# The last norm of a hybrid decoder step: scale per token at the eviction, and the second MLP's input written row by row

## The chip, the cores and the metric

The kernel runs on one core of a Trainium2 chip. TensorE (PE) multiplies, VectorE (DVE), ScalarE (ACT) and GpSimd (POOL) work on elements, SyncE (SP) issues most of the DMAs. The metric is the time of one execution on the device in microseconds; lower is better.

## The reference

One inference step of a decoder with two layers, 512 prompt tokens and 8 sample tokens, model width 1024, MLP width 4096. Layer 0 mixes with a gated linear recurrence, layer 1 with sparse attention. What the change touches is the MLP of layer 1 and the final norm:

```python
def rmsnorm(x, g):
    xf = x.astype(jnp.float32)
    y = xf * lax.rsqrt(jnp.mean(xf * xf, axis=-1, keepdims=True) + RMS_EPS)
    return (y * g.astype(jnp.float32)).astype(x.dtype)

def sq_relu_mlp(h, w_up, w_down):
    return jnp.square(jax.nn.relu(h @ w_up)) @ w_down

# per layer:
x = x + o                                             # o: the mixer's output
x = x + sq_relu_mlp(rmsnorm(x, norm_mlp[l]), w_mlp_up[l], w_mlp_down[l])
# at the end:
return rmsnorm(x, norm_final), ...
```

## The kernel before, in words

The stream x lies transposed in SBUF: 128 partitions, KD = 8 rows, N = 520 columns. Row k holds features 128k to 128k+127, a column is a token (512 of the prompt, 8 samples). A sum over the features of a token is thus a sum over rows and partitions.

A dense product (dense, L869; chunk_products, L858) goes by chunks of 128 output features. TensorE takes slabs of 2 MB of weights from stream, which SP loads two ahead, and adds up over the input rows in PSUM, in two halves of 260 columns; even chunks use banks 0 and 1, odd ones banks 2 and 3 (pair, L116). A matmul of float32 is two records in the trace. chunk_ready counts finished chunks, chunk_taken those that VectorE has taken out. The second MLP's up product has 32 chunks of 8 rows, the down product 8 chunks of 32 rows; both run in loops on TensorE and VectorE.

A norm goes as follows. residual (L1962) adds a chunk to its row of x on VectorE. Behind each row ScalarE writes its square into scratch (norm_act, L1447); GpSimd adds the squares of the first seven rows into the first (squares_added, L685); TensorE multiplies that row and the last one with a matrix of ones (norm_sum, L843), so that each partition holds the sum of every token in banks 6 and 7. ScalarE takes the root of mean plus eps (L1462), VectorE its reciprocal over 128 by 520 elements (norm_dve, L1825): rstd. At an MLP the product runs on rows that carry the gain alone (gained, L1442), and rstd is applied when the product is evicted (squared_relu, L1973). The rows with the gain are written by ScalarE either behind each square ("early", the first MLP) or all eight behind the last square ("late", the second MLP, into h, which the output projection nsa_out still reads until its last chunk).

At the end VectorE writes h = x * gain * rstd (L2314). TensorE turns h by 128 by 128 transposes, 4 to a PSUM bank, into token-major tiles (L1422; u counts 8 tiles: four blocks of 128 tokens, first for features 0 to 511, then for 512 to 1023; banks 0 to 3 in turn), the samples by 8 more (L1425). VectorE evicts even tiles (L2319), ScalarE odd ones (L1796). SP issues the first half of the output when four tiles are out, the second when eight are, then the samples (L613 to L621).

Each engine runs its own list in order and waits on semaphores; the order is written out by hand.

## Time and profile before

| what | value |
|---|---|
| median of 3 runs | 2174.71 us (2173.55 to 2177.26) |
| the profiled execution's own time | 2175.39 us |
| its span, first to last instruction | 2173.6 us |
| mean granted clock of TensorE | 0.967 |
| PE busy | 2030.5 us (93%) |
| DVE, ACT, POOL busy | 611.9, 404.6, 362.3 us (28%, 19%, 17%) |
| chain that ended last: TensorE's share | 85% |

The span is what the trace covers; the time of a run holds a little around it. The chain is followed back from the last instruction, at each step to what released it. A granted clock of 1.00 is 2.4 GHz, of 0.50 is 1.2 GHz. A page's line gives source line, engine, operation, tiles written and read.

### The profile page before, as it was taken

To read this page: it belongs to the slowest core of one execution; us is meant where nothing else is said; L and a number is where in the kernel's file an instruction comes from. 1 tells how busy PE (TensorE), PEld (TensorE's weight loads), DVE (VectorE), ACT (ScalarE), POOL (GpSimd) and SP (SyncE) were. 2 spreads that over 40 slices of the span, in tenths; PEclk is the share of its full clock that TensorE was granted. 3 is DMA by queue.
4 is the path that set the end of the run, shared out by engine and by line. 5 is a ranking of instruction groups with operands and counts; after the bars stand their busy time and mean duration, and the time that the engine had idled before them with its cause. 6 is when DMAs were issued, how large, how long until landed. Compare 5 with 4: busy or idle time off the path is not lost.

```text
span 2173.6 us, 28193 instructions
## 1 busy us (share of the span) xinstructions
PE 2030.5 (93%) x11084; PEld 1694.9 (78%) x11084; DVE 611.9 (28%) x1085; ACT 404.6 (19%) x839; POOL 362.3 (17%) x575
## 2 busy tenths in 40 slices
PE   7999998899999999999779999799849999999997
PEld 6888887788888888888656668687428788888886
DVE  3555456212211000011237753334401222110002
ACT  3343444210000000100225533233300100000000
POOL 2323234100000000000036654341011000000000
PEclk9999999899999999999859999899979999999999
DMA  5322232012222223215350009887991122212221
GB/s 137 87 62 63 68 100 70 22 66 77 77 77 77 77 77 77 77 43 193 73 143 2 2 1 221 183 184 202 293 323 70 39 77 77 69 47 77 77 77 39
DMA packets 213834, 206.83 MB, mean 95 GB/s; under 512 B 13906, under 2 KB 167107, under 8 KB 213603
## 3 DMA queue, kind: packets, MB, share of 16 engines
q1 hardware_dynamic: 195970, 186.84, 30.9%
q10 hardware_dynamic: 16416, 14.95, 2.1%
q0 software_dynamic: 1344, 3.67, 0.5%
q8 instruction: 64, 1.05, 0.2%
q14 instruction: 40, 0.32, 0.1%
HBM read 194.33 MB, written 18.42 MB: 98 GB/s over the span
## 4 chain that ended last, share of the span: by engine, by line
PE 85%; DVE 3%; SPq 3%; DMA 3%; ACTq 2%; issue 2%; ACT 2%; POOL 1%; DVEq 0%; POOLq 0%
PE ps L865 52%; PE ps L904 11%; PE ps L1083 4%; PE ps L1076 2%; PE ps L944 2%; DMA stream<-in_cache_nsa_kv 2%; PE ps L919 1%; PE ps L1137 1%; PE ps L1159 1%; ACTq L1715 1%; PE ps L1177 1%; PE ps L1285 1%; ACTq L347 1%; PE ps L970 1%; SPq L562 1%
## 5 line engine op out<-in xcount | busy, mean ns | idle before, releaser
L865 PE MATMUL ps<-h,stream 128*128 128x260 f32 x2688 | 593.4, 384 | 5.8 <-ACT h L1444 4.1
L865 PEld LDWEIGHTS ps<-h,stream 128*128 128x128 f32 x2688 | 512.8, 191 | 85.9 <-issue 4.7
L865 PE MATMUL ps<-big,stream 128*128 128x260 f32 (+1 forms) x2464 | 544.6, 384 | 4.7 <-DVE big L1981 3.9
L865 PEld LDWEIGHTS ps<-big,stream 128*128 128x128 f32 (+1 forms) x2464 | 468.0, 190 | 81.0 <-issue 5.1
L904 PE MATMUL ps<-h,stream 128*128 128x260 f32 x1024 | 237.0, 386 | 5.1 <-DVE h L1836 5.1
L904 PEld LDWEIGHTS ps<-h,stream 128*128 128x128 f32 x1024 | 191.7, 192 | 37.2 <-issue 10.0
L1453 ACT ACTIVATE scratch<-x 128x520 f32<-128x520 f32 x32 | 20.4, 637 | 1039.0 <-DVE x L1969 1039.0
L692 POOL TENSOR_TENSOR scratch<-scratch 128x520 f32<-128x520 f32 x24 | 30.9, 1285 | 995.8 <-ACT scratch L1453 995.8
L1969 DVE TENSOR_TENSOR x<-x,ps 128x520 f32 x32 | 22.3, 696 | 538.5 <-PE ps L865 522.8
L1978 DVE SCALAR_TENSOR_TENSOR scratch<-ps,rstd 128x520 f32<-128x520 f32 x64 | 44.8, 700 | 344.8 <-PE ps L865 344.8
L1083 PE MATMUL ps<-big 128*128 128x256 f32 x384 | 99.7, 383 | 0.0
L722 POOL COPY scratch<-stream 128x512 f32<-128x512 f32 (+1 forms) x72 | 43.2, 616 | 257.2 <-DMA stream<-big 157.4
L2151 DVE COPY big<-ps 128x512 f32<-128x512 f32 x80 | 55.3, 691 | 101.1 <-PE ps L1076 77.3
L1635 ACT ACTIVATE big<-ps,scratch 128x128 f32<-128x128 f32 (+3 forms) x128 | 66.3, 526 | 84.8 <-DVE scratch L2072 84.8
L746 POOL TENSOR_SCALAR big<-big,scratch 128x128 f32<-128x128 f32 (+3 forms) x128 | 77.2, 613 | 26.1 <-DVE scratch L2078 26.1
L1883 DVE COPY_PREDICATED scratch<-scratch,ps 128x512 f32<-128x512 int32 x64 | 47.0, 735 | 122.0 <-PE ps L944 100.6
L1685 ACT ACTIVATE big<-ps 128x512 f32<-128x512 f32 x81 | 48.4, 597 | 129.8 <-PE ps L1076 93.5
L1083 PEld LDWEIGHTS ps<-big 128*128 128x128 f32 x384 | 66.0, 192 | 5.4 <-DVE big L2151 0.3
L944 PEld LDWEIGHTS ps<-scratch 128*128 128x128 f32 x448 | 59.8, 199 | 9.8 <-POOL scratch L676 5.2
L944 PE MATMUL ps<-scratch 128*128 128x128 f32 x448 | 62.7, 285 | 3.7 <-POOL scratch L676 3.7
L675 POOL TENSOR_TENSOR scratch<-scratch,stream 128x256 f32<-128x256 f32 x56 | 46.0, 822 | 115.3 <-ACT stream L1521 101.2
L1076 PE MATMUL ps<-ident,scratch 128*128 128x128 f32 (+1 forms) x288 | 45.8, 288 | 16.8 <-POOL scratch L722 16.7
(311 smaller groups left out, 2000.4 us busy)
## 6 DMA issues: line engine op xcount, KB each, us to landing
stream<-in_w_mlp_up SPq DMA_DIRECT2D x16, 2048.0 KB, 7.6
stream<-in_w_mlp_down SPq DMA_DIRECT2D x16, 2048.0 KB, 9.0
stream<-in_cache_nsa_kv SPq DMA_DIRECT2D x128, 256.0 KB, 6.1
stream<-in_w_hgrn_in SPq DMA_DIRECT2D x32, 512.0 KB, 7.0
stream<-in_cache_nsa_kv SPq DMA_DIRECT2D x114, 128.0 KB
stream<-in_cache_nsa_kv ACTq DMA_DIRECT2D x114, 128.0 KB
stream<-in_cache_win_kv SPq DMA_DIRECT2D x16, 512.0 KB
out<-in_cache_win_kv SPq DMA_DIRECT2D x8, 1022.0 KB
```

The lines of the kernel that those rows point to most:

```text
L675: nc.gpsimd.tensor_tensor(lv[:, :, 0, :], kv[:, :, 0, :], ev[:, :, 0, :], ALU.mult)
L746: nc.gpsimd.tensor_scalar(probs, probs, wts[u % 4][:, br:br + 1], gtok[:, t, gate:gate + 1], ALU.mult, ALU.mult).then_inc(pa["probs"], 1)
L865: m = nc.tensor.matmul(pair(c)[0:n1, a, :], w[:, k, P * c_local:P * c_local + n1], rhs[:, k, NH * a:NH * a + NH], start=(k == 0), stop=(k ...
L904: m = nc.tensor.matmul(pair(c)[:, a, :], w[:, k, :], h[:, k, NH * a:NH * a + NH], start=(k == 0), stop=(k == KD - 1))
L944: m = nc.tensor.matmul(ps[:, 5 - l % 2, P * c:P * c + P], Lv[l % 2][:, P * c:P * c + P], Lv[l % 2][:, P * c:P * c + P], start=True, stop=True)
L1076: m = nc.tensor.transpose(ps[:, bank, P * g:P * g + n], src[0:n, g, :], ident[0:n, 0:n])
L1083: m = nc.tensor.matmul(ps[:, bank, 0:G * n // 2], W1[kv][:, kk, :, :].rearrange("p a n -> p (a n)"), columns(par), start=(rp == 0 and par ...
L1635: m = nc.scalar.activation(Pb[u % 4][:, br, 0:w], ps[:, 2 * a + br, 0:w], ACT.Exp, bias=nmax[a][:, br:br + 1], accum_out=sums[u % 4][:, br ...
L1685: nc.scalar.activation(out, ps[:, TB[s % 3], :], ACT.Copy).then_inc(sm["ev0"], 1)
L1883: nc.vector.copy_predicated(AT.rearrange("p (c t) -> p c t", c=TT), masks[:, mask:mask + 1, :].to_broadcast([P, TT, P]).bitcast(I32), ps[: ...
L1978: nc.vector.scalar_tensor_tensor(out=halves(Mz[p]), in0=pair(c), scalar=0.0, in1=halves(rstd[:]), op0=ALU.max, op1=ALU.mult).then_inc(relu ...
L2151: nc.vector.tensor_copy(out, ps[:, TB[s % 3], :]).then_inc(sm["ev1"], 1)
```

## The change

For the second MLP, the rows with the gain are written behind each square, into a buffer of their own in scratch (mlp_in), which the up product reads in place of h. The squares no longer lie in eight rows of scratch but in one row that gathers the sum, a ring of two, and one for the last row; ScalarE therefore waits, from the fourth row on, until GpSimd has added the row before last (square_taken).

For the final norm, the rows with the gain alone are written into h behind each square. TensorE sums the squares with the row of squares as the stationary operand and one column of ones, so that the sum of a token stands on the partition of that token (4 columns for the prompt's blocks, one for the samples): first for the row that GpSimd has added up, then for the last. VectorE copies the first into SBUF and adds the second, ScalarE takes the root, VectorE the reciprocal, of 128 by 4 and 8 by 1 elements. The transposes wait for the rows of h alone; tiles 0 to 3 go to banks 4 to 7, tiles 4 to 7 to banks 2, 3, 0, 1. The scale of a token is applied when its tile is evicted, and the samples' eviction is split between VectorE and ScalarE.

```diff
--- before.py
+++ after.py
@@ -256,6 +256,11 @@
         out_count = {"mix0": KD, "mlp0": 2 * KD, "kv": 3 * KD, "attn": 4 * KD, "mlp1": 5 * KD, "final": 6 * KD}
         squares = scratch[:, 0:KD * N].rearrange("p (k t) -> p k t", k=KD)
         squares_in = big[:, 12:12 + KD, :]
+        mlp_in = scratch[:, 0:KD * N].rearrange("p (k t) -> p k t", k=KD)
+        sq_total, sq_last = scratch[:, KD * N:KD * N + N], scratch[:, at_end - 5 * T + 2 * N:at_end - 5 * T + 3 * N]
+        sq_ring = [scratch[:, KD * N + N * n:KD * N + N * n + N] for n in range(1, 3)]
+        square_rows = [sq_total] + [sq_ring[k % 2] for k in range(1, KD - 1)] + [sq_last]
+        token_rstd = small[:, 0:TT + 1]
 
         per_head = {
             "in_min": 1, "in_sp": 1, "lf": 1, "f": 1, "th": 1, "g": 1, "scan": 1, "k": 1, "dend": 1, "d": 7, "take": 8,
@@ -300,7 +305,13 @@
         block = ctx.enter_context(nc.Block())
 
         hready = sem("hready")
-        ydone, ysdone = [sem("ydone0"), sem("ydone1")], sem("ysdone")
+        ydone, ysdone = [sem("ydone0"), sem("ydone1")], [sem("ysdone0"), sem("ysdone1")]
+        square_taken, token_scale = sem("square_taken"), sem("token_scale")
+        token_part, token_added = sem("token_part"), sem("token_added")
+
+        def y_bank(u):
+            return 4 + u if u < TT else (2 + u - TT) % 4
+
         yturned = sem("yturned")
         yrows = big[:, 0:8, :].rearrange("p k t -> p (k t)")[:, 0:TT * D].rearrange("p (a n) -> p a n", a=TT)
         ysrows = big[0:B, 8:10, :].rearrange("p k t -> p (k t)")[:, 0:D]
@@ -617,7 +628,8 @@
                     sp.wait_ge(ydone[p], TT // 2 * (half + 1))
                 sp.dma_start(y_prompt[0].rearrange("(a p) n -> p a n", p=P)[:, :, D // 2 * half:D // 2 * half + D // 2],
                              yrows[:, :, D // 2 * half:D // 2 * half + D // 2]).then_inc(stored, 16)
-            sp.wait_ge(ysdone, 1)
+            for p in range(2):
+                sp.wait_ge(ysdone[p], 1)
             sp.dma_start(y_sample.rearrange("b a n -> (b a) n"), ysrows).then_inc(stored, 16)
             for p in range(2):
                 sp.wait_ge(s0_out[p], 16 * heads // 2)
@@ -817,7 +829,14 @@
                     page, = page_numbers(mybir.EngineType.Pool, first_page(i, j) + 3, 1)
                     nc.gpsimd.dma_start(kv_tile(i)[:, j, 3, :], page_rows(i, j, page)).then_inc(pool_in[kv_slot(i)], 16)
 
-            squares_added("mlp1")
+            n = turn_of["mlp1"]
+            pool.wait_ge(norm["sq"], n * KD + 1)
+            for k in range(1, KD - 1):
+                pool.wait_ge(norm["sq"], n * KD + k + 1)
+                m = nc.gpsimd.tensor_tensor(sq_total, sq_total, square_rows[k], ALU.add)
+                m.then_inc(square_taken, 1)
+                pool.wait_ge(square_taken, k)
+            pool.sem_inc(norm["added"], 1)
             squares_added("final")
 
 
@@ -1404,23 +1423,46 @@
             pe.wait_ge(hready, 8)
             pe.wait_ge(pa["out"], UNITS)
             dense("nsa_out", 2, h, KD, 512)
-            norm_sum("mlp1", squares)
+            n = turn_of["mlp1"]
+            pe.wait_ge(norm["added"], n)
+            for a in range(2):
+                nc.tensor.matmul(ps[:, 6 + a, 0:NH], ones[:], sq_total[:, NH * a:NH * a + NH], start=True, stop=False)
+            pe.wait_ge(norm["sq"], n * KD + KD)
+            for a in range(2):
+                m = nc.tensor.matmul(ps[:, 6 + a, 0:NH], ones[:], sq_last[:, NH * a:NH * a + NH], start=False, stop=True)
+            m.then_inc(norm["sum"], 1)
             pe.wait_ge(norm["out"], out_count["mlp1"])
-            dense("up1", 8, h, KD, 512, turns=4)
+            dense("up1", 8, mlp_in, KD, 512, turns=4)
             for p in range(2):
                 pe.wait_ge(chunk_taken[p], taken(p, chunk_base["down1"]))
             dense("down1", 8, big, KF, P, turns=4)
-            norm_sum("final", squares)
-
+            def token_sums(k):
+                for a in range(TT + 1):
+                    n1 = min(P, N - P * a)
+                    m = nc.tensor.matmul(ps[0:n1, k % 2, a:a + 1], squares[:, k, P * a:P * a + n1], ones[:, 0:1],
+                                         start=True, stop=True)
+                return m
+
+            n = turn_of["final"]
+            pe.wait_ge(norm["added"], n)
+            pe.wait_ge(chunk_taken[0], taken(0, chunk_base["down1"] + KD))
+            token_sums(0).then_inc(token_part, 1)
+            pe.wait_ge(norm["sq"], n * KD + KD)
+            token_sums(KD - 1).then_inc(norm["sum"], 1)
+
+            pe.wait_ge(norm["out"], out_count["final"] - 1)
             for u in range(2 * TT):
                 a, cg = u % TT, u // TT
-                if a == 0:
-                    pe.wait_ge(norm["out"], out_count["final"] - KD // 2 * (1 - cg))
-                if u >= 4:
-                    pe.wait_ge(ydone[u % 2], (u - 4) // 2 + 1)
+                if u == TT:
+                    pe.wait_ge(norm["out"], out_count["final"])
+                    pe.wait_ge(chunk_taken[1], taken(1, chunk_base["down1"] + KD))
+                    pe.wait_ge(token_added, 1)
                 for c in range(4):
-                    m = nc.tensor.transpose(ps[:, u % 4, P * c:P * c + P], h[:, 4 * cg + c, P * a:P * a + P], ident[:])
+                    m = nc.tensor.transpose(ps[:, y_bank(u), P * c:P * c + P], h[:, 4 * cg + c, P * a:P * a + P], ident[:])
                 m.then_inc(yturned, 1)
+            for p in range(2):
+                pe.wait_ge(ydone[p], 1)
             for c in range(KD):
                 m = nc.tensor.transpose(ps[0:B, 4 + c // 4, P * (c % 4):P * (c % 4) + P], h[:, c, T:N], ident[:])
             m.then_inc(yturned, 1)
@@ -1789,12 +1831,33 @@
                     for c in range(3):
                         load_page(i, j, c)
 
-            norm_act("mlp1", squares, added("nsa_out"), late=[(GAIN_MLP + KD, h)])
-            norm_act("final", squares, added("down1"))
+            n, wait_row = turn_of["mlp1"], added("nsa_out")
+            for k in range(KD):
+                wait_row(k)
+                if 3 <= k < KD - 1:
+                    act.wait_ge(square_taken, k - 2)
+                nc.scalar.activation(square_rows[k], x[:, k, :], ACT.Square).then_inc(norm["sq"], 1)
+                gained(GAIN_MLP + KD, mlp_in, k)
+            act.wait_ge(norm["sum"], n + 1)
+            nc.scalar.activation(halves(rstd[:]), ps[:, 6:8, 0:NH], ACT.Sqrt, bias=eps[:], scale=1.0 / D)\
+                .then_inc(norm["sqrt"], 1)
+
+            n, wait_row = turn_of["final"], added("down1")
+            for k in range(KD):
+                wait_row(k)
+                nc.scalar.activation(squares[:, k, :], x[:, k, :], ACT.Square).then_inc(norm["sq"], 1)
+                gained(GAIN_FINAL, h, k)
+            act.wait_ge(token_added, 1)
+            nc.scalar.activation(token_rstd[0:B, TT:TT + 1], token_rstd[0:B, TT:TT + 1], ACT.Sqrt, bias=eps[0:B], scale=1.0 / D)
+            nc.scalar.activation(token_rstd[:, 0:TT], token_rstd[:, 0:TT], ACT.Sqrt, bias=eps[:], scale=1.0 / D)\
+                .then_inc(norm["sqrt"], 1)
+            act.wait_ge(token_scale, 1)
             for u in range(1, 2 * TT, 2):
                 act.wait_ge(yturned, u + 1)
-                nc.scalar.activation(yrows[:, u % TT, 512 * (u // TT):512 * (u // TT) + 512], ps[:, u % 4, :], ACT.Copy)\
-                    .then_inc(ydone[1], 1)
+                nc.scalar.activation(yrows[:, u % TT, 512 * (u // TT):512 * (u // TT) + 512], ps[:, y_bank(u), :], ACT.Copy,
+                                     scale=token_rstd[:, u % TT:u % TT + 1]).then_inc(ydone[1], 1)
+            act.wait_ge(yturned, 2 * TT + 1)
+            nc.scalar.activation(ysrows[:, D // 2:D], ps[0:B, 5, :], ACT.Copy, scale=token_rstd[0:B, TT:TT + 1]).then_inc(ysdone[1], 1)
 
 
         @block.vector
@@ -2309,17 +2372,23 @@
             norm_dve("mlp1")
             squared_relu("up1")
             residual("down1")
-            norm_dve("final")
-            for k in range(KD):
-                nc.vector.scalar_tensor_tensor(out=h[:, k, :], in0=x[:, k, :],
-                                               scalar=vec[:, GAIN_FINAL + k:GAIN_FINAL + k + 1], in1=rstd[:],
-                                               op0=ALU.mult, op1=ALU.mult).then_inc(norm["out"], 1)
+            dve.wait_ge(token_part, 1)
+            nc.vector.tensor_copy(token_rstd[0:B, TT:TT + 1], ps[0:B, 0, TT:TT + 1])
+            ch.link(nc.vector.tensor_copy(token_rstd[:, 0:TT], ps[:, 0, 0:TT]))
+            dve.wait_ge(norm["sum"], turn_of["final"] + 1)
+            nc.vector.tensor_tensor(token_rstd[0:B, TT:TT + 1], token_rstd[0:B, TT:TT + 1], ps[0:B, 1, TT:TT + 1], ALU.add)
+            nc.vector.tensor_tensor(token_rstd[:, 0:TT], token_rstd[:, 0:TT], ps[:, 1, 0:TT], ALU.add).then_inc(token_added, 1)
+            dve.wait_ge(norm["sqrt"], turn_of["final"] + 1)
+            nc.vector.reciprocal(token_rstd[0:B, TT:TT + 1], token_rstd[0:B, TT:TT + 1])
+            ch.link(nc.vector.reciprocal(token_rstd[:, 0:TT], token_rstd[:, 0:TT]))
+            dve.sem_inc(token_scale, 1)
             for u in range(0, 2 * TT, 2):
                 dve.wait_ge(yturned, u + 1)
-                nc.vector.tensor_copy(yrows[:, u % TT, 512 * (u // TT):512 * (u // TT) + 512], ps[:, u % 4, :])\
-                    .then_inc(ydone[0], 1)
+                nc.vector.tensor_scalar(yrows[:, u % TT, 512 * (u // TT):512 * (u // TT) + 512], ps[:, y_bank(u), :],
+                                        token_rstd[:, u % TT:u % TT + 1], None, ALU.mult).then_inc(ydone[0], 1)
             dve.wait_ge(yturned, 2 * TT + 1)
-            nc.vector.tensor_copy(ysrows.rearrange("p (c n) -> p c n", c=2), ps[0:B, 4:6, :]).then_inc(ysdone, 1)
+            nc.vector.tensor_scalar(ysrows[:, 0:D // 2], ps[0:B, 4, :], token_rstd[0:B, TT:TT + 1], None, ALU.mult)\
+                .then_inc(ysdone[0], 1)
 
 
 # ---- launch: one core; inputs and outputs as the reference has them ----
```

ScalarE's list from the last chunks of nsa_out to the first square of the down product, before (scratch takes the squares):

```order
L1453 ACTIVATE scratch<-x 128x520 [waits chunk_taken1]
L1453 ACTIVATE scratch<-x 128x520 [waits chunk_taken0]
L1444 ACTIVATE h<-x,vec 128x520 x8
L1462 ACT_TABLE_LOAD
L1462 ACTIVATE rstd<-ps,eps 128x520 [waits norm_sum]
L1453 ACTIVATE scratch<-x 128x520 [waits chunk_taken1]
```

And after, where scratch takes the squares and, with vec as second operand, the rows with the gain:

```order
L1839 ACTIVATE scratch<-x 128x520 [waits square_taken,chunk_taken0]
L1486 ACTIVATE scratch<-x,vec 128x520
L1839 ACTIVATE scratch<-x 128x520 [waits square_taken,chunk_taken1]
L1486 ACTIVATE scratch<-x,vec 128x520
L1839 ACTIVATE scratch<-x 128x520 [waits chunk_taken0]
L1486 ACTIVATE scratch<-x,vec 128x520
L1842 ACT_TABLE_LOAD
L1842 ACTIVATE rstd<-ps,eps 128x520 [waits norm_sum]
L1848 ACTIVATE scratch<-x 128x520 [waits chunk_taken1]
L1486 ACTIVATE h<-x,vec 128x520
```

The eight scaled rows that stood together behind the last square now stand one behind each square, and the squares from the fourth to the seventh wait for square_taken too.

VectorE's list from the end of the last product's loop to the end of the kernel, before:

```order
L1964 COMPARE_AND_BRANCH
L1827 RECIPROCAL rstd<-rstd 128x520 [waits norm_sqrt,chunk_taken1,chunk_taken0]
L2314 SCALAR_TENSOR_TENSOR h<-x,vec,rstd 128x520 [waits dve_chain]
L2314 SCALAR_TENSOR_TENSOR h<-x,vec,rstd 128x520 x7
L2319 COPY big<-ps 128x512 [waits yturned] x4
L2322 COPY big<-ps 8x1024 [waits yturned]
```

And after (stream is the buffer that holds the small per-token numbers):

```order
L2027 COMPARE_AND_BRANCH
L2376 COPY stream<-ps 8x1 [waits token_part,chunk_taken1,chunk_taken0]
L2377 COPY stream<-ps 128x4
L2379 TENSOR_TENSOR stream<-stream,ps 8x1 [waits norm_sum,dve_chain]
L2380 TENSOR_TENSOR stream<-stream,ps 128x4
L2382 RECIPROCAL stream<-stream 8x1 [waits norm_sqrt]
L2383 RECIPROCAL stream<-stream 128x4
L2387 TENSOR_SCALAR big<-ps,stream 128x512 [waits dve_chain,yturned]
L2387 TENSOR_SCALAR big<-ps,stream 128x512 [waits yturned] x3
L2390 TENSOR_SCALAR big<-ps,stream 8x512 [waits yturned]
```

The reciprocal over 520 columns and the eight scaled rows are gone; six instructions on one or four columns stand in their place, and the evictions read a scale.

TensorE's list from the end of the last product, before:

```order
L854 MATMUL ps<-scratch,ones 128x260 [waits norm_added]
L854 MATMUL ps<-scratch,ones 128x260
L854 MATMUL ps<-scratch,ones 128x260 [waits norm_sq]
L854 MATMUL ps<-scratch,ones 128x260
L1422 MATMUL ps<-ident,h 128x128 [waits norm_out]
L1422 MATMUL ps<-ident,h 128x128 x15
L1422 MATMUL ps<-ident,h 128x128 [waits ydone0,norm_out]
L1422 MATMUL ps<-ident,h 128x128 x3
L1422 MATMUL ps<-ident,h 128x128 [waits ydone1]
```

And after:

```order
L1443 MATMUL ps<-ones,scratch 128x1 [waits chunk_taken0,norm_added]
L1443 MATMUL ps<-ones,scratch 128x1 x3
L1443 MATMUL ps<-ones,scratch 8x1
L1443 MATMUL ps<-ones,scratch 128x1 [waits norm_sq]
L1443 MATMUL ps<-ones,scratch 128x1 x3
L1443 MATMUL ps<-ones,scratch 8x1
L1462 MATMUL ps<-ident,h 128x128 [waits norm_out]
L1462 MATMUL ps<-ident,h 128x128 x15
L1462 MATMUL ps<-ident,h 128x128 [waits token_added,chunk_taken1,norm_out]
L1462 MATMUL ps<-ident,h 128x128 x15
L1467 MATMUL ps<-ident,h 8x128 [waits ydone1,ydone0]
L1467 MATMUL ps<-ident,h 8x128 x7
```

The sums are ten matmuls of one column, in place of four of 260; of the transposes, none waits for an eviction except those of the samples.

## Rows read from the trace of the kernel before

**Rows 1.** The chain of waits, 1690 us to the end: start us, us, what.

```profile
1690.92 0.64 ACT scratch L1453
1691.56 4.96 ACT h L1444 x8
...
1696.84 226.39 PE ps L865 x1024
...
1925.14 226.39 PE ps L865 x1024
...
2152.41 0.65 ACT scratch L1453
...
2153.09 1.16 PE ps L854 x4
...
2154.28 0.70 ACT rstd L1462
...
2155.46 3.41 DVE rstd L1827
...
2158.90 2.79 DVE h L2314 x4
...
2161.73 5.31 PE ps L1422 x32
```

**Rows 2.** Timeline, first MLP and second: start us, us, instruction [idle before <-releaser].

```profile
460.41 0.64 ACT L1453 ACTIVATE scratch<-x 128x520 f32<-128x520 f32 x1 [5.76 <-DVE x L1969]
460.95 0.71 ACT L1444 ACTIVATE h<-x,vec 128x520 f32<-128x520 f32 x1
461.10 1.15 PE L854 MATMUL ps<-scratch,ones 128*128 128x260 f32 x4 [0.70 <-ACT scratch L1453]
462.08 8.30 PE L865 MATMUL ps<-h,stream 128*128 128x260 f32 x37
469.31 0.70 DVE L1978 SCALAR_TENSOR_TENSOR scratch<-ps,rstd 128x520 f32<-128x520 f32 x1 [2.11 <-PE ps L865]
...
1705.84 0.70 DVE L1978 SCALAR_TENSOR_TENSOR scratch<-ps,rstd 128x520 f32<-128x520 f32 x1 [3.79 <-PE ps L865]
```

**Rows 3.** Stretches: us, then each engine's busy us; PEclk, DMA share, GB/s.

```profile
462.00:464.00 2.00, 2.00 (x11) 1.77 (x10) 0.20 (x1) 1.66 (x2) 0.00 (x0) 1.00 1.05 401
...
1696.80:1698.00 1.20, 1.16 (x3) 0.97 (x4) 0.00 (x0) 1.19 (x2) 0.00 (x0) 0.61 0.00 0
...
1925.20:1927.00 1.80, 1.80 (x6) 1.45 (x7) 0.00 (x0) 0.00 (x0) 0.00 (x0) 0.65 1.13 333
...
2161.70:2163.70 2.00, 1.97 (x9) 1.98 (x10) 2.00 (x4) 0.00 (x0) 0.00 (x0) 0.50 0.00 0
2164.70:2166.70 2.00, 2.00 (x19) 1.80 (x18) 1.60 (x4) 1.09 (x2) 0.00 (x0) 1.00 0.00 0
2166.60:2172.40 5.80, 1.31 (x13) 0.87 (x10) 1.90 (x2) 0.80 (x2) 0.00 (x0) 0.92 1.00 367
```

**Rows 4.** Timeline of SyncE, the issues of the output's two halves.

```profile
2165.82 2.31 SPq L618 DMA_DIRECT2D out<-big  x2
```

**Rows 5.** Groups by line and shape: xcount | busy us, mean ns | idle before.

```profile
L1010 PE MATMUL ps<-big,stream 128*128 128x1 f32 x128 | 15.1, 248 | 0.0
...
L944 PE MATMUL ps<-scratch 128*128 128x128 f32 x448 | 62.7, 285 | 3.7 <-POOL scratch L676 3.7
...
L985 PE MATMUL ps<-ident,scratch 128*128 128x128 f32 x32 | 4.8, 272 | 0.0
...
L1433 ACT ACTIVATE lnb<-lnb 128x8 f32<-128x8 f32 x1 | 0.2, 209 | 9.4 <-DVEq L1810 9.4
...
L1843 DVE TENSOR_SCALAR big<-ps 128x520 f32<-128x520 f32 x8 | 5.5, 694 | 4.8 <-PE ps L904 4.8
...
L2078 DVE RECIPROCAL scratch<-scratch 128x2 f32<-128x2 f32 x64 | 10.6, 165 | 23.4 <-POOL scratch L741 21.3
...
L692 POOL TENSOR_TENSOR scratch<-scratch 128x520 f32<-128x520 f32 x24 | 30.9, 1285 | 995.8 <-ACT scratch L1453 995.8
```

## The prediction

> **What bounds the kernel now.** I read the chain of waits from its end backwards, then the timeline of the two places that the change touches, then the granted clock there, and last the durations of single instructions.
>
> The chain [rows 1] shows TensorE as the bound nearly everywhere: the second MLP's two products take 226.39 us each without a break (1024 records each, so 0.221 us a record, and with 32 chunks 7.07 us a chunk). Two stretches on it have no product running, and the change is about these.
>
> The first lies before the second MLP. The last residual row is squared at 1690.92; then ScalarE writes all eight rows of the MLP's input (4.96 us), and only at 1696.84 does TensorE start [rows 1]. The first MLP of the kernel, at 460 us, has the other order: there each row of input is written right behind its square, so that behind the last square one row is left. Square at 460.41, product at 462.08 [rows 2]. That is the very form the change brings to the second MLP, so the trace of before shows its price.
>
> The second is the end. Behind the last square at 2152.41 come: sums by TensorE (1.16), square root (0.70), reciprocal over 520 columns (3.41), eight rows scaled, of which the first four must be there (2.79), 32 transposes (5.31), with their evictions [rows 1]. The first half of the output is issued at 2165.82 [rows 4]. From 2166.6 to 2172.4 the DMA share is 1.00 at 367 GB/s [rows 3]: 2.1 MB of output at that rate are 5.8 us, that is, the tail is full of transfer from the moment that the first half is issued, and the span ends 2173.6 - 2165.8 = 7.8 us after that issue. So what the end is worth is read from one instant: when the first half is issued.
>
> **The change, part by part.** Times are those of the profiled execution, span 2173.6, its own time 2175.39; that is 0.7 over the median of the runs (2174.71).
>
> *Inputs of the second MLP.* Seven of eight scaled rows leave the stretch behind the last square; they stand behind the seven earlier squares, where ScalarE has 7.07 us a chunk and needs 0.64 + 0.71 [rows 1, 2]. The new buffer lets these rows be written while the products of the output projection still read h. The added wait of ScalarE on GpSimd's additions costs nothing: rows come 7.07 us apart, an addition takes 1.29 [rows 5], and three rows may be open; behind the waiting square stands only that chunk's scaled row. The price is read off the first MLP: from last square to first eviction of the up product 469.31 - 460.41 = 8.90 us; in the second 1705.84 - 1690.92 = 14.92 us [rows 1, 2]. Difference 6.02. It has two parts. The start: 1.67 against 5.92, that is 4.25. And the clock: in the first MLP TensorE pauses 0.70 us before the sums and stays at 1.00 (2.4 GHz); in the second it has been idle since its sums (they end 1.84 us behind the square by the first MLP's rows, so at 1692.8) and is granted 0.61 in the first 1.2 us of the product [rows 2, 3], and the first chunk takes 1.8 us longer. I take all 6.0. Bounds: 4.25 if the clock falls here as well, 6.0 if not. The reciprocal is late next: sums, table, root and 3.41 us of reciprocal begin as early as in the first MLP, where the first eviction waited for the product, not for it.
>
> *The last norm.* The scaled rows (plain gains now, without the norm) move behind each square, where a chunk of the down product is 226.39 / 8 = 28.3 us long: nothing on the path. The seven earlier rows are summed while the last product still runs. What is left behind the last square's end, 2153.05:
> - token sums of the last row: 5 matmuls of one column, 10 records at 15.1 / 128 = 0.118 us [rows 5], with the start 1.3 us: 2154.4;
> - two small additions, two small square roots, two small reciprocals: four on VectorE at 0.165, two on ScalarE at 0.21 [rows 5], with three handovers of some 0.05: 1.2 us: 2155.6. Before, VectorE issued its reciprocal 0.48 us after the root's end at 2154.98 [rows 1]; I leave 0.4 for such a late issue: 2156.0;
> - meanwhile TensorE goes on from the sums into the transposes, which need only the plain rows, into banks that are free. At full clock 19 records fall in 2.0 us [rows 3], 0.105 each: 16 of them, and the drain, end at 2156.4, so that the third and fourth tile are there before their evictions are due;
> - evictions with the scale per token: VectorE 0.70 (a scaled copy from PSUM, [rows 5]), for ScalarE I take the 0.71 of a row scaled from SBUF [rows 2]. Two each: 2157.4, first half issued at 2157.5.
>
> That is 2165.8 - 2157.5 = 8.3 us earlier. The second half follows 1.5 us later, within the 2.9 us of transfer of the first, and the samples' rows (8 transposes and two evictions of eight partitions) come 2 to 3 us behind the first issue, still under the transfer: the tail keeps its 7.8 us. The removed reciprocal over 520 columns and the eight scaled rows on VectorE lay wholly on the path, the transposes too; they now lie beside the chain or are gone.
>
> The bounds of this part: 9 us if VectorE issues without the 0.4 and a hand-over is shorter; 5.5 us if sums and transposes all run at half clock (sums 2.6, transposes 0.22 each [rows 3], first issue at 2160.3).
>
> Of the clock in this stretch the rows speak both ways. After the pause of 0.7 us before the sums of the first MLP the product went on at 1.00 [rows 2, 3]; after the pause of 1.9 us between the two products of the second MLP (1696.84 + 226.39 = 1923.23 to 1925.14) they ran at 0.65 in the mean of 1.8 us [rows 1, 3]. After the change there are a pause of 0.7 and one-column matmuls on both sides of it. I take the full clock, and keep the fall as a rival. The transposes themselves ran at 0.50 after the long pause and were granted 1.00 while nothing but transposes was issued [rows 3]. The Trainium skill says otherwise ("TensorE: Matmul & The Clock Gate", Part 4: PE-mode transpose): the full clock does not engage for transposes. The row of 2164.7 to 2166.7 does not agree. By the page's rule the first issue would come at 2158.8, and the sum would be 1.3 us less.
>
> **Sum.** 6.0 + 8.3 = 14.3: 2175.4 - 14.3 = 2161.1 in the profiled execution's terms, 2160.4 against the median of the runs. I forecast 2161.0, between these.
>
> **Rivals.**
> - *The clock falls in the last stretch,* or VectorE's first instructions behind its loop come late. For it: the fall after 1.9 us, and the late issue of 0.48. Against it: 1.00 after the pause of 0.7. Price 1.3 (transposes alone at half clock: 16 at 0.22 from 2154.4, with drain and eviction, issue at 2158.8) to 2.8 (sums too): 2162.3 to 2163.8.
> - *The clock falls at the second MLP all the same:* 1.8 of the 6.0 is lost, 2162.8. The first MLP is the same sequence and shows 1.00 [rows 3].
> - *The up product becomes slower, and with it the kernel.* TensorE now streams its input from scratch, where VectorE writes the rectified rows at the same time, and not from h. It decides from 14.3 / 1024 = 14 ns a record; from 18 ns the kernel is slower by over 0.2%. For it: matmuls from scratch in the first layer took 285 ns in the mean where those with the identity took 272 [rows 5], 13 ns, with other engines writing there; that alone would give 2174.4, twice that 2187.7. Against it: the product from h, beside which VectorE writes scratch and big, and the one from big, beside which it writes x, take the same 226.39 to the digit [rows 1].
> - *No change that can be told:* only if 10 of the 14 us fail to come; the scratch rival at its half is the one way that I see.
>
> **How the numbers follow.** Forecast 0.58, the clock or a late issue in the last stretch 0.33, the clock at the second MLP 0.05, the slower product 0.04, of which half ends on the slow side. The forecast's own range, with 1.5 us of spread for a median of few runs (those of before lie between 2173.55 and 2177.26), is 2159 to 2163; with the first rivals 2158.3 to 2164.6, which leaves out under 2 in 10. Faster by over 0.2% (4.3 us, about what a measurement of this kernel can tell from no change) 0.96, within 0.2% 0.02, slower 0.02.
>
> **What would show it.** Second MLP: one scaled row on the chain behind the last square, its product within 2 us of that square, granted 1.00, and 226.4 us long; a longer product means the scratch rival. End: the first output issue 8 us closer to the last square than the 13.4 of before; the chain there going square, sums, small steps, evictions, DMA; transposes beginning at the end of the sums. A clock of 0.5 between the sums and the last transpose means the first rival. The forecast is wrong if the DMA tail takes longer than 7.8 us behind its first issue, or if the stretch up to 1690 us moves, where no instruction has changed.

## The result, and the profile after

The changed kernel took 2156.64 us (median of 4 runs, 2155.37 to 2161.49), the kernel before on the same chip 2174.19 (4 runs, 2173.55 to 2177.26): ratio 0.992, 95% interval 0.9906 to 0.9934. It is faster, by 17.6 us where 13.7 were forecast against the median shown (2174.71 to 2161.0); 2156.64 lies 2.4 below the forecast's own range (2159 to 2163) and 1.7 below the wider one (from 2158.3).

The profiled execution of the changed kernel took 2157.23, span 2155.6, mean granted clock 0.968, PE busy 2027.9 us (94%). Its chain of waits, in the stretches that [rows 1] show of before (start us, us, what):

```profile
1687.80 0.65 ACT scratch L1839
...
1688.48 1.14 PE ps L1432 x4
1689.63 224.46 PE ps L884 x1024
...
1916.00 224.70 PE ps L884 x1024
...
2140.85 0.71 DVE x L2032
2141.56 0.14 issue
2141.69 2.26 PE ps L1443 x20
2143.95 5.31 PE ps L1462 x32
```

Three things are to be seen against [rows 1]. From the last square to the up product it is now 1.83 us (5.92 before), and that product takes 224.46 (226.39). The down product takes 224.70 (226.39), though nothing of it was changed. And at the end the scaled rows, the long reciprocal and the matrix of ones are gone; token sums and transposes alone are left. But the last square itself comes at 1687.80 and not at 1690.92, behind instructions that are the same in both kernels.

The clock in these stretches (us, then each engine's busy us; PEclk, DMA share, GB/s), beside [rows 3]:

```profile
1689.60:1691.60 2.00, 2.00 (x11) 1.74 (x10) 0.41 (x1) 1.45 (x2) 0.00 (x0) 1.00 0.00 0
1916.00:1918.00 2.00, 2.00 (x9) 1.77 (x10) 0.00 (x0) 0.00 (x0) 0.00 (x0) 1.00 1.15 322
2141.60:2144.00 2.40, 2.31 (x21) 2.25 (x22) 0.22 (x2) 1.23 (x2) 0.00 (x0) 1.00 0.00 0
2144.40:2148.00 3.60, 3.60 (x20) 3.60 (x19) 1.83 (x5) 1.76 (x4) 0.00 (x0) 0.53 0.02 5
2148.60:2154.40 5.80, 1.53 (x15) 1.08 (x12) 1.54 (x3) 1.88 (x3) 0.00 (x0) 1.00 1.00 367
```

Both products of the second MLP begin at 1.00. Behind the token sums the transposes run at 0.53: the clock fell there, so 32 of them take 5.31 us as before. The last row is the output's transfer, full at 367 GB/s as before.

The timeline of SyncE answers to [rows 4], and that of ScalarE shows what the first half of the output waited for (start us, us, instruction [idle before <-releaser]):

```profile
2147.80 2.63 SPq L629 DMA_DIRECT2D out<-big  x2
```

```profile
2141.58 0.64 ACT L1848 ACTIVATE scratch<-x 128x520 f32<-128x520 f32 x1 [26.82 <-DVE x L2032]
...
2144.50 0.28 ACT L1852 ACTIVATE stream<-stream,eps 128x4 f32<-128x4 f32 x1
2145.40 0.69 ACT L1857 ACTIVATE big<-ps,stream 128x512 f32<-128x512 f32 x1 [0.61 <-PE ps L1462]
2147.05 0.69 ACT L1857 ACTIVATE big<-ps,stream 128x512 f32<-128x512 f32 x1 [0.96 <-PE ps L1462]
```

From the end of the last square (2142.22) to the first issue are 5.58 us; they were 12.77 (2153.05 to 2165.82). The second of ScalarE's two evictions waited 0.96 us for a transpose at half clock: that is the wait which now ends last. Behind the issue the span ends 7.80 us later (2155.6 - 2147.8), as before.

So the 18.0 us between the two spans come apart like this:

| stretch | before | after | gain | in the forecast |
|---|---|---|---|---|
| up to the last square before the second MLP | 1690.92 | 1687.80 | 3.1 | 0 |
| that square to the start of the down product | 234.22 | 228.20 | 6.0 | 6.0 |
| down product | 226.39 | 224.70 | 1.7 | 0 |
| its end to the first output issue | 14.29 | 7.10 | 7.2 | 8.3 |
| first issue to the end | 7.8 | 7.8 | 0 | 0 |

What has to be explained is two gains that no changed instruction made (4.8 together), and 1.1 us missing at the end.

### The profile page after: what moved, and what is told of

It is laid out like the page before. It is cut to its first block, busy times and chain, and to the rows that moved or that the text cites. A ratio compares the mean times of both kernels' runs of the same rounds, so it can differ in the third digit from the quotient of the medians.

```text
span 2155.6 us, 28235 instructions
## 1 busy us (share of the span) xinstructions
PE 2027.9 (94%) x11096; PEld 1692.9 (79%) x11096; DVE 603.6 (28%) x1082; ACT 410.3 (19%) x849; POOL 362.4 (17%) x575
## 4 chain that ended last, share of the span: by engine, by line
PE 85%; SPq 3%; DVE 3%; DMA 3%; ACTq 2%; issue 2%; ACT 1%; POOL 1%; DVEq 0%; POOLq 0%
PE ps L884 52%; PE ps L923 11%; PE ps L1102 4%; PE ps L1095 2%; PE ps L963 2%; DMA stream<-in_cache_nsa_kv 2%; ACTq L1757 1%; PE ps L938 1%; PE ps L1156 1%; PE ps L1178 1%; PE ps L1196 1%; PE ps L1304 1%; ACTq L358 1%; SPq L573 1%; PE ps L989 1%
## 5 line engine op out<-in xcount | busy, mean ns | idle before, releaser
L884 PE MATMUL ps<-h,stream 128*128 128x260 f32 x1664 | 367.0, 384 | 1.7 <-DVE h L2368 1.7
L884 PEld LDWEIGHTS ps<-h,stream 128*128 128x128 f32 x1664 | 317.1, 191 | 51.1 <-DVE h L2368 1.9
L923 PE MATMUL ps<-h,stream 128*128 128x260 f32 x1024 | 237.0, 386 | 5.1 <-DVE h L1899 5.1
L884 PE MATMUL ps<-scratch,stream 128*128 128x260 f32 x1024 | 224.6, 382 | 0.0
L923 PEld LDWEIGHTS ps<-h,stream 128*128 128x128 f32 x1024 | 191.7, 192 | 37.3 <-issue 10.0
L884 PEld LDWEIGHTS ps<-scratch,stream 128*128 128x128 f32 x1024 | 194.5, 190 | 30.0 <-issue 0.2
L704 POOL TENSOR_TENSOR scratch<-scratch 128x520 f32<-128x520 f32 x18 | 23.2, 1287 | 915.6 <-ACT scratch L1495 490.5
L1495 ACT ACTIVATE scratch<-x 128x520 f32<-128x520 f32 x16 | 10.2, 637 | 482.9 <-DVE x L2032 482.9
L1848 ACT ACTIVATE scratch<-x 128x520 f32<-128x520 f32 x8 | 5.1, 636 | 441.7 <-DVE x L2032 441.7
```

The source lines that it names most:

```text
L884: m = nc.tensor.matmul(pair(c)[0:n1, a, :], w[:, k, P * c_local:P * c_local + n1], rhs[:, k, NH * a:NH * a + NH], start=(k == 0), stop=(k ...
L923: m = nc.tensor.matmul(pair(c)[:, a, :], w[:, k, :], h[:, k, NH * a:NH * a + NH], start=(k == 0), stop=(k == KD - 1))
```

## Experiments

**Each half alone (E1, E2), and the changed kernel again.** E1 has the new second MLP and the old last norm, E2 the reverse (lines against the changed kernel, cut):

```diff
# E1: last norm as before
-            token_sums(0).then_inc(token_part, 1)
...
-            token_sums(KD - 1).then_inc(norm["sum"], 1)
+            norm_sum("final", squares)
# E2: second MLP as before
-            dense("up1", 8, mlp_in, KD, 512, turns=4)
+            dense("up1", 8, h, KD, 512, turns=4)
...
+            norm_act("mlp1", squares, added("nsa_out"), late=[(GAIN_MLP + KD, h)])
```

> Only the second MLP's part of the change: its inputs written behind each square; the last norm as before. Theory A (the time is the sum of the two edits, and what else the two traces differ by is chance of single executions): 6.0 us faster than before (4.3 from the earlier start of the up product, 1.8 from a clock that stays at 1.00 there), so 2168.2. Theory B (the change as a whole also quickens the stretch ahead of 1690 us or the down product, by 3 to 5 us, in every execution): 9 to 11 us faster if this part brings it, 6.0 if not. In its trace: up product 224.5 us, starting within 2 us of the last square; the last square of the output projection at 1690.9 by B's denial, at 1687.8 by B.

> Only the last norm's part: sums per token, scale at the eviction; the second MLP's inputs all behind the last square, as before. Theory A: 7.2 us faster than before (14.0 us from the last square to the end of the span against 21.2), so 2167.0, up to 8.5 where the clock does not fall in the transposes. Theory B: 10 to 12 us faster if this part brings the rest, 7.2 if neither alone does and only both together do. Up product 226.4 us as before, with the fall of the clock at its start.

> The changed kernel once more, with a new profile. Theory A (chance): the last square of the output projection lies anywhere between 1687 and 1692 us, as in the other runs whose instructions up to there are the same; the pause of 1.9 us between up and down product is followed by a low clock in some executions (down product 226.4) and not in others (224.7); the time against before 13.5 to 17.5 us faster. Theory B: 1687.8 and 224.7 again, 17.5 us faster.

On one chip, beside the kernel before at 2173.77 (16 runs, 2169.89 to 2177.93): E1 2166.62 (9 runs; ratio 0.9963, 0.9951 to 0.9974), E2 2166.54 (6 runs; 0.9968, 0.9957 to 0.998), the changed kernel 2159.1 (5 runs, 2156.44 to 2161.3; 0.9935, 0.9922 to 0.9947). The halves gain 7.15 and 7.23, 14.4 together; the whole gains 14.7. They add up as far as intervals of two to three us either way can tell. E1 alone does not decide between the theories: its last square came at 1686.38, the sign of theory B, and its interval, 5.7 to 10.7 us, holds A's 6.0 and reaches into B's 9 to 11. The changed kernel's second trace decides it for A, with a late square and a long down product:

```profile
1689.82 0.65 ACT scratch L1839
...
1691.65 224.46 PE ps L884 x1024
...
1918.02 226.39 PE ps L884 x1024
```

E1's chain, second MLP and the start of the old last norm:

```profile
1688.21 224.46 PE ps L877 x1024
...
1914.58 224.70 PE ps L877 x1024
...
2142.81 0.40 issue
2143.21 3.42 DVE rstd L1856
```

The up product from scratch takes 224.46 here too: the rival of a slower product has fallen. E2's end of chain:

```profile
2151.82 0.71 DVE x L2008
2152.53 0.14 issue
2152.66 2.26 PE ps L1429 x20
2154.92 5.22 PE ps L1448 x32
```

It is the same as in the changed kernel, with its first issue at 2159.19, 7.37 behind the last residual add (6.95 in the first trace of the changed kernel, 7.34 in the second, 14.14 before).

**Token sums before the last eviction (E3).** The 20 records of token sums stand in one piece, behind a wait for the residual add. Ten of them, of the first seven rows, were to run before it. They waited because the last chunk of the down product lies in banks 0 and 1 and the sums were written there. E3 puts them into banks 2 and 3, which are free a chunk earlier, and the late tiles into 0 to 3 in the other order:

```diff
-            return 4 + u if u < TT else (2 + u - TT) % 4
+            return 4 + u if u < TT else u - TT
...
-                    m = nc.tensor.matmul(ps[0:n1, k % 2, a:a + 1], squares[:, k, P * a:P * a + n1], ones[:, 0:1],
+                    m = nc.tensor.matmul(ps[0:n1, 2 + k % 2, a:a + 1], squares[:, k, P * a:P * a + n1], ones[:, 0:1],
```

> The changed kernel with one thing moved: the first token sums go to bank 2 and the last to bank 3, in place of banks 0 and 1, which the last chunk of the down product holds until VectorE has added it; tiles 4 to 7 go to banks 0 to 3. If the wait for that bank is what put both token sums on the path, TensorE starts the first ones right behind the product and the two are no longer one piece of 2.26 us: 0.8 to 1.1 us faster than the changed kernel, where the clock is the same in both. If the sums were hidden anyway, or the fall of the clock sets the transposes whatever the sums do, the same within 0.3 us.

2159.18 (6 runs; 0.9936, 0.9923 to 0.995): the same as the changed kernel beside it. TensorE's timeline:

```profile
2142.43 1.07 PE L1443 MATMUL ps<-ones,scratch 128*128 128x1 f32 x10
2144.18 1.18 PE L1443 MATMUL ps<-ones,scratch 128*128 128x1 f32 x10 [0.67 <-ACT scratch L1848]
2145.29 5.31 PE L1462 MATMUL ps<-ident,h 128*128 128x128 f32 x32
```

The first ten now stand right behind the product, as meant, but the transposes still take 5.31 us, and from residual add to first issue it is 6.89 (6.95). From the end of the product to the first issue it is 7.04 (7.10 to 7.49 in the changed kernel). The six runs spread too widely to tell a gain of 0.8; by the trace the bank was the reason of that wait, but not what the end was waiting for: that was the clock, as the next experiment shows.

**The clock held up by matmuls that nobody reads (E4, E4b).** E4 is E3 with two full matmuls behind the early sums; their result goes to bank 6, which nobody reads. E4b has two more ahead of the sums:

```diff
+            def keep_busy(count, row):
+                for n in range(count):
+                    nc.tensor.matmul(ps[:, 6, 0:NH], ones[:], row, start=True, stop=True)
...
             token_sums(0).then_inc(token_part, 1)
+            keep_busy(2, big[:, 20, 0:NH])
```

> The early sums of the run before, and two matmuls of 260 columns that no one reads between the first and the last token sums (0.9 us of TensorE, in a pause of 0.7: the last sums come some 0.25 us later). Theory C: the low clock in the transposes comes from the pause and the one-column matmuls ahead of them, and hides what the early sums gain. Then with the pause filled the clock holds 1.00 at least in a part of the executions, the transposes take 3.6 us in place of 5.2, the first output issue comes 6 us behind the last addition in place of 6.9, and the kernel is 0.5 to 1 us faster than the changed one. Theory D: the clock has no part in it, the evictions set the end: the same or 0.25 us slower.

> As the run before with two more such matmuls right behind the last product, ahead of the first token sums: TensorE is then busy with wide matmuls in 1.8 of the 3 to 4 us ahead of the transposes, and the last sums come 1.1 us later. Theory C: granted clock 1.00 from the product to the last transpose, transposes 3.5 us, first issue some 6.6 us behind the last addition. Theory D: transposes at 0.50 for part of the way as in the four traces with the new norm, first issue at 8.

E4's chain:

```profile
2144.29 0.91 PE ps L1448 x10
2145.20 1.07 PE ps L913 x4
2146.28 0.91 PE ps L1448 x10
2147.19 3.64 PE ps L1468 x32
```

Its first output issue, by SyncE's timeline:

```profile
2149.88 2.12 SPq L629 DMA_DIRECT2D out<-big  x2
```

The clock in the two stretches, sums and transposes:

```profile
2144.30:2147.20 2.90, 2.90 (x24) 2.70 (x25) 0.91 (x3) 1.25 (x2) 0.00 (x0) 1.00 0.01 3
2147.20:2150.80 3.60, 3.60 (x34) 3.56 (x35) 2.80 (x8) 2.55 (x5) 0.00 (x0) 1.00 0.02 5
```

All 32 transposes run at 1.00 in 3.64 us, and from the end of the product to the first issue it is 5.59 (2149.88 - 2144.29) where the changed kernel needs 7.10 to 7.49. So 1.5 to 1.9 us of the end were the clock and the bank together, and 1.45 of it came with the two filling matmuls (7.04 in E3): theory C. They fill the pause and stand among the one-column matmuls at once, so which of the two brings the fall is not separated. The Trainium skill says that the full clock does not engage for transposes ("TensorE: Matmul & The Clock Gate", Part 4: PE-mode transpose); the second row does not agree, since nothing but transposes was issued in it.

The time shows little of this: E4 2157.28 (5 runs; 0.9922, 0.991 to 0.9935), E4b 2158.19 (one run). The two further matmuls of E4b buy nothing: transposes 3.65, from the product's end to the first issue 6.47. E4's profiled execution took 2159.29, 2 us more than that of the changed kernel, because its last square before the second MLP came at 1691.37. What varies there hides what is gained here.

**The pause between the products (E5), and the kernel before again.** In [rows 3] the clock fell behind the 1.9 us pause between up and down product. E5 fills it, in both layers alike, with three matmuls that nobody reads (the second layer's is shown):

```diff
             dense("up1", 8, mlp_in, KD, 512, turns=4)
+            keep_busy(3, big[:, 0, 0:NH])
```

> The changed kernel with three matmuls of 260 columns that no one reads (1.3 us) in the pause of 1.9 us between up and down product of both MLPs. Theory E: whether the clock falls behind that pause is chance of the execution, 1.7 us each time (seen in 4 of 6 traces at each of the two places). Filled, the down products take 224.7 us in every execution, the clock never falls there, and the kernel is 2.3 us faster in the mean than the changed kernel (2 places x 1.7 x 4 of 6). If the fall has another cause than the pause, the same.

> The kernel before once more, for a second trace. Theory A (the stretch up to the last square of the output projection differs by chance): anywhere between 1686 and 1692 us. Theory B (the new second MLP quickens it): 1690.9 or later again, as in the two traces with the old second MLP, against 1686.4 to 1689.8 in the four with the new one.

E5: 2157.14 (6 runs, 2154.65 to 2163.41; 0.9934, 0.9919 to 0.9948). In its trace the clock falls behind neither up product, and the down product takes 224.70. The 2.3 us of theory E do not show in the times: the changed kernel was not run beside it, and its ratio to before was 0.9935 both in its second and in its third measurement. Nor are the runs closer together: the slowest two (2162.36 and 2163.41) had a mean granted clock of 0.966 and 0.964 over the whole execution, the fastest three 0.971. Either the fill does not hold in every execution or the clock, and the time with it, varies elsewhere as well; with one trace that is open. Without a fill the fall is a matter of the single execution. Over ten traces without it, the pause in the second layer was followed by a low clock and a down product of 226.38 or 226.39 us in six (both of before, E2, the changed kernel's second, E3, E4b), and by 1.00 and 224.69 or 224.70 in four (the changed kernel's first and third, E1, E4). In the first layer, where not one instruction was touched and the pause is 2.0 us, it fell in eight of the ten (not in E1 and E3).

The kernel before, taken again, has its last square at 1689.33, which theory B excluded, and a time of 2174.24.

**All three together (E6), beside the changed kernel a third time.** E6 has E3's banks, E4's two matmuls, E5's three (the first line below stands behind up0 and behind up1):

```diff
+            keep_busy(3, big[:, 0, 0:NH])
...
             token_sums(0).then_inc(token_part, 1)
+            keep_busy(2, big[:, 20, 0:NH])
```

> The three pieces of E3, E4 and E5 together: token sums into banks 2 and 3, two filling matmuls behind the sums of the first seven rows, three filling matmuls in the pause between up and down product of both layers. Theory A (the granted clock is what is left to gain behind the change): TensorE at 1.00 from the first MLP to the last transpose; the down product 224.5 to 224.7 in every execution (226.4 where the clock falls), 32 transposes 3.64 and not 5.3, from the end of the down product to the first output issue 5.5 and not 6.9 to 7.3. Against the changed kernel on the same chip 1.3 from the end and 1 to 2 from the product boundary of the second layer, 0 to 2 from that of the first: 2.3 to 4 us less, median some 2155.5 if the changed kernel has 2158.5. Theory B (the pieces overlap, or each filling matmul costs what it gives back): within 1 us of the changed kernel.

> The changed kernel unchanged, a third time, beside E6 on the same chip. If the unchanged stretch in front of the second MLP differs by chance from execution to execution: last square of the output projection anywhere between 1685 and 1691.5, the median between 2156 and 2160. If the change itself moved that stretch forward by 3 us: square below 1689.

E6 2155.72 (6 runs, 2154.09 to 2159.54; 0.9917, 0.9904 to 0.993), the changed kernel 2161.09 (6 runs, 2156.38 to 2162.44; 0.9935, 0.9922 to 0.9949), the kernel before 2174.96 (11 runs). Between the means of six runs each, 2156.36 and 2160.52, lie 4.2 us; the runs' own spread (standard deviations 2.0 and 2.2) gives an interval of 1.5 to 6.9, or a ratio of 0.9981, 0.9968 to 0.9993. That is a little above the 2.3 to 4 us of theory A, with an interval that holds them; theory B, within 1 us, is out. The changed kernel's own median, 2161.09, lies above the 2156 to 2160 expected of it. E6 has the lowest ratio to before; E4's (0.9922) cannot be told from it. Its chain and clock:

```profile
1689.03 224.46 PE ps L884 x1024
...
1915.40 224.69 PE ps L884 x1024
2140.09 0.91 PE ps L1450 x10
2141.00 1.07 PE ps L913 x4
2142.07 0.91 PE ps L1450 x10
2142.98 3.64 PE ps L1470 x32
```

```profile
2140.10:2143.00 2.90, 2.90 (x24) 2.70 (x25) 0.91 (x3) 1.25 (x2) 0.00 (x0) 1.00 0.04 8
2143.00:2146.60 3.60, 3.60 (x34) 3.56 (x35) 2.80 (x8) 2.55 (x5) 0.00 (x0) 1.00 0.00 1
```

The product's end is followed by the sums without a pause, and the first issue comes at 2145.68, 5.59 behind it. Which share of the 4.2 us is the end (1.5 to 1.9 by the traces), which the two product boundaries and which chance, the times do not tell: between the two traces the last square before the second MLP alone differs by 3.3 us (1687.20 and 1690.49).

**Where the unchanged stretch differs.** In the changed kernel the last square before the second MLP came at 1687.80, 1689.82 and 1690.49 in its three traces, in the kernel before at 1690.92 and 1689.33, in all twelve traces between 1685.09 and 1691.37. The ranges overlap, and the changed kernel's second and third trace lie in that of before: a gain of 3 us by the change in every execution would have shown in them, and did not; a smaller one is not ruled out. One source of the differences is the first layer: in the four traces in which the clock did not fall there (E1, E3, E5, E6) the square comes at 1685.09 to 1688.03, in the eight in which it fell at 1687.72 to 1691.37. Another is the sparse attention. TensorE's waits in it, 1540 to 1632 us, of before, of the changed kernel's first trace and of its third (engine line waited for: us, times, longest):

```profile
PE ps L1395 <- DMA stream<-in_cache_nsa_kv: 27.9, 7, 9.5
PE ps L1379 <- DMA stream<-out: 4.6, 2, 2.4
PE ps L1285 <- DMA stream<-in_cache_nsa_kv: 1.9, 1, 1.9
```

```profile
PE ps L1414 <- DMA stream<-in_cache_nsa_kv: 23.2, 6, 9.3
PE ps L1304 <- DMA stream<-in_cache_nsa_kv: 3.8, 2, 1.9
PE ps L1398 <- DMA stream<-out: 3.0, 1, 3.0
```

```profile
PE ps L1414 <- DMA stream<-in_cache_nsa_kv: 26.1, 6, 9.6
PE ps L1398 <- DMA stream<-out: 4.4, 2, 3.7
PE ps L1304 <- DMA stream<-in_cache_nsa_kv: 1.9, 2, 1.7
```

Together they come to 34.4, 30.0 and 32.4 us. Between before and the changed kernel's first trace the 3.1 us arise here: L1285 (L1304 behind the change) begins on TensorE at 1491.36 and 1491.51, the product behind the attention at 1631.96 and 1628.84. Between the changed kernel's first and third trace only a part does: in the third these instants are 1493.44 and 1631.66, so that 1.9 of 2.8 us lie ahead of the waits. There the granted clock differs, 0.90 and 0.84 from 1130 to 1150 us. Why these loads land earlier or later, and why the clock differs, was not tried.

## Why the prediction was wrong, and where it was right

*Second MLP, 6.0: right in both parts.* Square to product 5.92 to 1.83 (4.09 for the 4.25 said, which set the first MLP's start in the timeline, 462.08, beside the second's in the chain; the chain of before has 462.24, below), product 226.39 to 224.46 (1.93 for 1.8), its start at 1.00 as in the first MLP. Its sign "226.4 us long" did not fit its own sum: with 1.8 gained from the clock the product had to be some 224.6. The rival in which the clock falls there happened in none of the nine traces with the new form.

*Scratch as the input: right.* The up product took 224.46 to 224.49 us in all nine traces in which it was read from scratch, and as long in the first MLP of before, where it is read from h and begins at 1.00 too:

```profile
462.24 224.46 PE ps L865 x1024
```

The 13 ns between matmuls of the first layer were no price of reading there.

*Last norm, 8.3: mis-sized; it gave 7.2.* The rival with 0.33, the clock falling in the last stretch, is what happened, in every trace of the new norm without a filling matmul in the end: from the end of the reciprocals (2145.05) to the first issue it is 2.75 us where 1.5 were forecast, because the evictions wait for transposes at half clock. It is not that transposes are granted no more: E4, E4b and E6 run the same 32 at 1.00. One step was wrong besides: "the seven earlier rows are summed while the last product still runs". The squares were, by GpSimd, but the token sums of that row waited in banks 0 and 1 for the last eviction, so both sums stand in one piece of 2.26 us and end 1.73 us behind the end of the last square, where 1.3 were forecast. The small steps took less than said (sums' end 2143.95 to the end of the reciprocals at 2145.05: 1.1 for 1.6). With the bank and the clock mended, E6 has 4.06 us between the end of the last square (2141.62) and the issue, where 4.45 were forecast: the sum had been worked out for a kernel that holds the full clock, and that kernel was two small edits away.

*The tail of 7.8: right* (7.80, in E2 7.81).

*The step that failed:* the range, by "1.5 us of spread for a median of few runs". It was read off three times of the kernel before, 3.7 us apart in all, and the sum took one trace of it as fixed where the change does not reach: the last square at 1690.92 and a down product of 226.39 were carried over, and a move of either was put at nothing. In the profiled execution they gave 3.1 and 1.7 us, against 1.1 missing at the end: 18.0 in place of 14.3. The repeats show both to be chance of the execution: the square comes anywhere within 6.3 us in twelve traces, by the first layer's clock, by the waits in the attention and by the clock there, and the clock behind each pause between products is worth 1.7 us. All sources of the spread are not known (E5). Of the first four runs three lay below 2157.3. The changed kernel's fifteen runs, over three measurements (medians 2156.64, 2159.1, 2161.09), lie between 2155.37 and 2162.44, with a standard deviation of 2.4 and a median of 2160.2, which is 0.8 below the forecast of 2161.0; nine of the fifteen lie within 2159 to 2163. Against the kernel before, whose medians were 2173.8 to 2175.0 each time, that is 14 us (17.6, 14.7 and 13.9 in the three measurements); the sum said 14.3. That nearness is partly luck: 7.2 stood in place of 8.3 at the end, and the clock at the product boundary, which fell in all three traces with the old second MLP and in three of seven with the new one (unfilled), gave part of it back. If that last difference is of the change (TensorE's pause of 4 us before the up product is gone) or of chance, so few traces do not settle; E1's gain of 7.15 where its instructions account for 6.0 would fit, but its interval (5.7 to 10.7) holds 6.0 too.

The condition set at the end, that the stretch up to 1690 us might move, is what was met; it was named and given no width.

## What to carry to other kernels

Before a range is drawn, read which waits in the unchanged part of the program depend on DMAs that land in no fixed time and behind which pauses the clock may fall, and give the median of a few runs that width, not the spread of three times. Where work is cut from a stretch without products, price what is left at both levels of the clock, and ask what TensorE does in each pause of it: here eight matmuls of 260 columns that nobody reads, with an exchange of banks, gave 4.2 us more in the mean (1.5 to 6.9), of which the traces show 1.5 to 1.9 at the end. When work is said to be hidden, look up which PSUM bank it writes and who has to leave that bank first.

## What the runs showed of the hardware

- In the six traces with one-column sums ahead of the transposes and no wide matmul among them (the changed kernel's three, E2, E3, E5) a pause of 0.7 to 1.0 us stood there too, and the granted clock fell to about half over most of the transposes (0.53 from 2144.4 to 2148.0 in the first). With two 260-column matmuls between the sums and no pause it stayed at 1.00 in all three traces (E4, E4b, E6). Pause and one-column matmuls were not tried apart.
- A pause of 1.9 to 2.0 us between the same two products was followed by a low clock in some executions and not in others (six of ten in the second layer, eight of ten in the first). Filled, it was not, at both places in the two traces with a fill (E5, E6).
- Transposes alone hold the full clock: 32 in 3.64 us at 1.00, against 5.31 where it fell.
- TensorE's waits for the same loads in the attention differ by 2.4 us in total between two executions of one program (30.0 and 32.4).
